# Expert mixer split by tokens: three of five token tiles go through the whole expert tables with matmuls, two tiles keep gathering their rows

## The reference

```python
def peer(h, w_q, subkeys, u_tab, v_tab):          # h: 640 tokens x 1024; u_tab, v_tab: 16384 x 1024
    q = (ht @ w_q).reshape(T, PEER_HEADS, 2, PEER_HALF)              # 8 heads x 2 x 128
    s = jnp.einsum('thpd,hpnd->thpn', q, subkeys)                    # 128 subkeys each
    s1, i1 = lax.top_k(s[:, :, 0], 16); s2, i2 = lax.top_k(s[:, :, 1], 16)
    cand = s1[..., :, None] + s2[..., None, :]; cidx = i1[..., :, None] * 128 + i2[..., None, :]
    sc, pos = lax.top_k(cand.reshape(T, 8, 256), 16)
    eidx = jnp.take_along_axis(cidx.reshape(T, 8, 256), pos, axis=-1); gate = jax.nn.softmax(sc, axis=-1)
    a = jax.nn.gelu(jnp.einsum('td,tkd->tk', xi, u_tab[ei]))         # k: 8 heads x 16 = 128 experts per token
    return jnp.einsum('tk,tkd->td', gi * a, v_tab[ei])
```

## Time and profile before

| | |
|---|---|
| median of three runs | 5233.46 us (5231.72 to 5237.55) |
| span of the profiled execution | 5232.4 us |
| granted TensorE clock, mean | 0.869 |
| bytes moved by DMA | 1482.66 MB, of them 1342.42 MB on the software queue (the gathers) |
| busy: PE, DVE, ACT, POOL | 75%, 58%, 21%, 60% |

### The profile page before, as it was taken

The page is one execution under the profiler, slowest core; times in us unless marked ns, Lnnn a source line. Parts: engine busy times, 40 slices in busy tenths (PEclk is TensorE's granted clock), DMA queues, the critical chain, the costliest instruction groups (busy, mean ns, idle before and its releaser), DMA issues. The chain is left out here.

```text
span 5232.4 us, 51066 instructions
## 1 busy us (share of the span) xinstructions
PE 3918.3 (75%) x11340; PEld 1901.7 (36%) x11340; DVE 3046.2 (58%) x6901; ACT 1093.8 (21%) x2566; POOL 3138.9 (60%) x2832
## 2 busy tenths in 40 slices
PE   8986787787787666676678898877787666766675
PEld 3544754333333222232233443533333223322232
DVE  2014744766666666666651552666666666667665
ACT  1002212212221222122211242222222221222222
POOL 0003603777777777777760331477777777777775
PEclk9998888898898888888888799888889888888888
DMA  4126017999999999999992401899999999999997
GB/s 159 58 64 175 4 36 267 387 364 361 362 362 359 354 356 358 359 357 353 356 346 77 121 1 32 315 381 365 363 363 354 359 358 364 356 353 359 357 359 302
DMA packets 525836, 1482.66 MB, mean 283 GB/s; under 512 B 52901, under 2 KB 162597, under 8 KB 525513
## 3 DMA queue, kind: packets, MB, share of 16 engines
q0 software_dynamic: 369216, 1342.42, 68.7%
q1 hardware_dynamic: 154352, 138.22, 8.2%
q10 hardware_dynamic: 2080, 0.01, 0.0%
HBM read 1476.98 MB, written 3.48 MB: 283 GB/s over the span
## 5 line engine op out<-in xcount | busy, mean ns | idle before, releaser
L1303 PE MATMUL ps<-arena,mod_scale 128*128 128x512 f32 x5120 | 2472.0, 645 | 1030.4 <-ACT mod_scale L1240 1027.8
L1303 PEld LDWEIGHTS ps<-arena,mod_scale 128*128 128x128 f32 x5120 | 1051.5, 208 | 2414.9 <-issue 2324.7
L1190 POOL DMA_INDIRECT arena<-in_peer_u,small x1280 | 1381.3, 1079 | 726.3 <-issue 377.8
L1194 POOL DMA_INDIRECT arena<-in_peer_v,small x1280 | 1503.0, 1174 | 470.1 <-issue 317.8
L1390 DVE CUSTOM_DVE_ANT_0 arena<-arena 128x1024 f32<-128x1024 f32 x1280 | 1518.2, 1223 | 412.7 <-DMA arena<-in_peer_u,small 290.7
L1240 ACT ACTIVATE mod_scale<-ident,tail 128x128 f32<-128x128 f32 x1280 | 391.4, 388 | 82.3 <-DVE tail L1400 82.3
L1400 DVE TENSOR_TENSOR tail<-tail,small 128x8 f32<-128x8 f32 x160 | 27.0, 169 | 500.6 <-ACT tail L1236 499.9
L268 POOL TENSOR_TENSOR arena<-arena 2x512 f32<-2x512 f32 x12 | 15.5, 1294 | 464.4 <-ACT arena L260 464.4
L1236 ACT ACT_TABLE_LOAD x80 | 102.6, 1283 | 864.1 <-DVE tail L1390 863.9
L1228 ACT ACTIVATE arena<-ps 128x256 f32<-128x256 f32 x80 | 30.6, 382 | 1073.7 <-PE ps L1293 1073.7
L1313 PE MATMUL ps<-hT 128*128 128x512 f32 x512 | 231.6, 606 | 11.6 <-DMA hT<-in_peer_w_q 11.6
(11 more groups left out here) (221 smaller groups left out, 3611.4 us busy)
## 6 DMA issues: line engine op xcount, KB each, us to landing
hT<-in_w_mod SPq DMA_DIRECT2D x144, 256.0 KB, 3.8
arena<-in_peer_u,small POOLq DMA_INDIRECT x1280, 6.3
arena<-in_peer_v,small POOLq DMA_INDIRECT x1280, 6.4
arena<-in_even_w_in SPq DMA_DIRECT2D x8, 2048.0 KB, 8.9
arena<-in_peer_w_q SPq DMA_DIRECT2D x8, 2048.0 KB, 11.6
hT<-in_peer_w_q SPq DMA_DIRECT2D x32, 512.0 KB, 15.0
arena<-in_w_mod SPq DMA_DIRECT2D x6, 2048.0 KB, 8.5
arena<-in_odd_w_in SPq DMA_DIRECT2D x3, 2048.0 KB, 14.1
```

Source lines behind the costliest of these rows:

```text
L1190: pool.indirect_dma_start(u_rows[:, j], None, u_table, at).then_inc(m.u_landed[j], 16)
L1194: pool.indirect_dma_start(v_rows[:, j], None, v_table, at).then_inc(m.v_landed[j], 16)
L1303: mm = pe.matmul(y_banks[b][:, c], diag[:, q, j], v_rows[:, j, c * 512:(c + 1) * 512], start=(q == 0 and j == 0), stop=(q == 1 and j == HA ...
```

## The change

Tiles 0 and 1 (256 tokens) keep the gathered way; tiles 2 to 4 (384 tokens, DENSE = 3) go through all 16384 experts. Per layer, in order:

- Queries of all five tiles are projected at the start, 16 chunks (`project`), then scored (`score`) and kept in SBUF. DVE chooses experts for tiles 0 and 1 (16 `choose`), then `decode` turns each tile's choices to indices and gates. The gathers start after decode(0).
- U pass, 128 steps in four stages of 32: SP loads expert tile i of u (128 experts, four transfers of 128 KB in pieces of 1 KB, three slots); DVE turns it with one 32x32-block transpose of 128x1024 (`turn`); PE multiplies it with hT of the 384 tokens (`dots_of`, 8 matmuls of 384 columns); ACT takes gelu and stores the 128x384 result to DRAM (`act_rows`). The model columns of u, w_q and hT are renumbered alike (`quarter`, `by_quarters`, `from_blocks`), so that the block transpose yields complete 128-row operands.
- Beside it, in stages 0 to 2 DVE chooses for tiles 2 to 4 (a head every four steps). In stages 1 to 3 the choices of a tile become a dense matrix of gates: DVE builds one-hot rows for 8 tokens (`one_hot`, two 128x1024 operations), ACT scales them (8 operations), PE multiplies them (8 matmuls of 128 columns), ACT copies the result out and stores 1 MB for each 16 tokens to DRAM (`gate_rows`); 48 such groups.
- V pass, 128 steps: SP loads v in tiles of 1 MB (two expert tiles), the stored acts (`w_in`, 768 KB for four expert tiles, pieces of 1.5 KB) and the stored gates (`g_in`, 1.5 MB for eight expert tiles, 3072 pieces of 512 B); DVE multiplies acts by gates (`weigh`, 128x384); PE accumulates 6 matmuls of 512 columns into six PSUM banks.
- The 256 picks of the gathered tiles are spread over both passes by `pace`: 1.5 per step in stage 0, 0.25 in stages 1 and 2, 1.5 in stage 3, 1.3 in the V pass; a v row follows 14 picks behind its u row. u has eight slots, v four. For tile 0 ACT scales the v row and POOL adds it; for tile 1 DVE does both in one operation (`add_row`). PE no longer takes part in them.
- The loops are written out; no register operands are left. In `modulate` of the second half the sum is written renumbered, and twice for tiles 0 and 1.

```diff
+LAG = 14
+def pace(i):
+    stage, r = divmod(i, STAGE)
+    if i < 0:
+        return 0
+    if stage == 0:
+        return max(0, 3 * (r - 1) // 2)
+    if stage in (1, 2):
+        return 45 + 8 * (stage - 1) + (r + 1) // 4
+    if stage == 3:
+        return 61 + 3 * (r + 1) // 2
+    return 109 + 13 * (i - STEPS + 1) // 10
+def picks_by(i):
+    return min(pace(i), P * GATHERED)
+def rows_by(i):
+    return max(0, min(pace(i - 1) - LAG, P * GATHERED))
...
-                        hold(pool, S.multiplied, 16 * n + 8 * q + j + 1 - SLOTS, S.pool_step)
+            pool.wait_ge(S.decoded, 1)
...
+            for k in range(PICKS + LAG):
+                if k + U_ROWS == P:
+                    pool.wait_ge(S.decoded, 2)
+                if k + U_ROWS < PICKS:
+                    pool.wait_ge(S.dotted, k + 1)
+                    u_gather(k + U_ROWS)
+                p = k - LAG
+                if p < 0:
+                    continue
...
+                elif p < P:
+                    pool.wait_ge(S.scaled, p + 1)
+                    c(pool.tensor_tensor(y_sum[:, 0], y_sum[:, 0], v_rows[:, p % V_ROWS], ALU.add))
+                else:
+                    pool.wait_ge(S.dve_added, p - P + 1)
+                if p + V_ROWS < PICKS:
+                    v_gather(p + V_ROWS)
...
+                    if g >= 2:
+                        sp.wait_ge(S.weighed, GBLOCK * (g - 1))
+                    sp.dma_start(g_in[:, g % 2].rearrange("p g i t -> p g (i t)"),
+                                 m.gate_rows[0:TG, :, g * GBLOCK:(g + 1) * GBLOCK, :].rearrange("g j i t -> j g (i t)"))\
+                        .then_inc(S.g_landed[g % 2], 16)
...
+                    if w >= 2:
+                        sp.wait_ge(S.tile_done, ABLOCK * (w - 1))
...
+                    sp.dma_start(w_in[w % 2],
+                                 m.act_rows[w * ABLOCK:(w + 1) * ABLOCK, :, 0:ND].rearrange("k j t -> j k t"))\
+                        .then_inc(S.w_in_landed[w % 2], 16)
+                if n >= 2:
+                    sp.wait_ge(S.tile_done, VBLOCK * (n - 1))
+                sp.dma_start(v_in[:, n % 2], v_dense[n]).then_inc(S.v_landed[n % 2], 16)
...
-                        mm = pe.matmul(y_banks[b][:, c], diag[:, q, j], v_rows[:, j, c * 512:(c + 1) * 512],
+                pe.wait_ge(S.u_ready, i + 1)
+                if i >= 4:
+                    pe.wait_ge(S.gelu_done, i - 3)
+                for k in range(KD):
+                    mm = pe.matmul(m.ps[:, i % 4, 0:ND], u_turned[:, i % 2, k], m.hT[:, k, N0:N], start=(k == 0),
+                                   stop=(k == KD - 1))
...
+            for k in range(TILES):
+                pe.wait_ge(S.weighed, k + 1)
+                pe.wait_ge(S.v_landed[k // VBLOCK % 2], 16 * (k // VBLOCK // 2 + 1))
+                for o in range(2 * DENSE):
+                    t, half = divmod(o, 2)
+                    mm = pe.matmul(m.ps[:, o, :], w_in[k // ABLOCK % 2][:, k % ABLOCK, t * P:(t + 1) * P],
+                                   v_in[:, k // VBLOCK % 2, k % VBLOCK, half * 512:(half + 1) * 512], start=(k == 0),
+                                   stop=(k == TILES - 1))
+                mm.then_inc(S.tile_done, 1)
...
-                    nc.scalar.activation(diag[:, q, j], m.ident[:], ACT.Copy, scale=weight[:, q, j:j + 1])\
+                nc.scalar.activation(y_sum[:, 0] if p == 0 else row, row, ACT.Copy, scale=weight[:, half % 2, j:j + 1])\
+                    .then_inc(S.scaled, 1)
...
+            def turn(i):
+                dve.wait_ge(S.u_landed[i % U_SLOTS], 64 * (i // U_SLOTS + 1))
+                if i >= 2:
+                    dve.wait_ge(S.dots_full, i - 1)
+                dve.transpose(u_turned[:, i % 2].rearrange("p c (m a) -> p m c a", m=4),
+                              u_raw[:, i % U_SLOTS].rearrange("p m (c b) -> p m c b", b=32)).then_inc(S.u_ready, 1)
...
+            def weigh(k):
+                w, g = k // ABLOCK, k // GBLOCK
+                dve.wait_ge(S.w_in_landed[w % 2], 16 * (w // 2 + 1))
+                dve.wait_ge(S.g_landed[g % 2], 16 * (g // 2 + 1))
+                to = w_in[w % 2][:, k % ABLOCK].rearrange("p (g t) -> p g t", t=STRIPE)
+                dve.tensor_tensor(to, to, g_in[:, g % 2, :, k % GBLOCK], ALU.mult).then_inc(S.weighed, 1)
...
+            for h in range(H):
+                if h == 5:
+                    turn(0)
+                    turn(1)
+                for t in range(GATHERED):
+                    choose(t, h, best[t])
+            for t in range(GATHERED):
+                decode(t, best[t])
+            for i in range(LAST):
+                if i + 2 < STEPS:
+                    turn(i + 2)
+                if i < STEPS:
+                    stage, r = divmod(i, STAGE)
+                    if stage >= 1 and r == 0:
+                        decode(GATHERED + stage - 1, best[0])
...
+                    if head_at(i) is not None:
+                        t, h = head_at(i)
+                        choose(GATHERED + t, h, best[0])
+                if STEPS - 2 <= i < 2 * STEPS - 2:
+                    weigh(i - STEPS + 2)
+                for half in halves_by(i - 2):
+                    weights(half)
+                for p in range(picks_by(i - 1), picks_by(i)):
+                    meet(p)
+                for p in range(max(P, rows_by(i - 1)), max(P, rows_by(i))):
+                    add_row(p)
```

More of the change, by code:

```diff
@@ L278, in modulate, with rows @@
     gain = m.arena[:, ARENA - D:ARENA]
+    scaled = m.arena[:, ARENA - 4 * D:ARENA - 2 * D].rearrange("p (b d) -> p b d", b=2)
+    turned = m.arena[:, ARENA - 6 * D:ARENA - 4 * D].rearrange("p (t d) -> p t d", t=GATHERED)
+    def rows(t):
+        return turned[:, t] if half == 1 and t < GATHERED else m.h[:, t]
     square = m.arena[:, ARENA - 2 * D:ARENA - D]
@@ new lines, in early, with groups_at, head_at @@
+            for q in range(4):
+                m.early.load(sp, i, slots[i][32 * q:32 * q + 32], quarter(a.peer_w_q[l], i, q))
+    return early
+STAGE = 32
+STEPS = 4 * STAGE
+def groups_at(i):
+    stage, r = divmod(i, STAGE)
+    if not 1 <= stage <= 3 or not 2 <= r < 28:
+        return range(0)
+    first = 16 * (stage - 1)
+    return range(first + 16 * (r - 2) // 26, first + 16 * (r - 1) // 26)
+def head_at(i):
+    stage, r = divmod(i, STAGE)
+    return (stage, r // 4) if stage < 3 and r % 4 == 1 else None
@@ L1196, in _ @@
-            pool.wait_ge(S.context_full, LOADS)
-            every(gathers)(pool)
-        @block.sync
-        def _(sp):
-            for n in range(2, LOADS):
-                sp.wait_ge(S.context_full, n - 1)
-                sp.dma_start(slots[n % 2], columns(a.peer_w_q[l], n)).then_inc(S.w_landed[n % 2], 16)
-            sp.wait_ge(S.context_full, LOADS)
-            sp.dma_start(w_later, w_q[:, :, 0]).then_inc(S.w_later_landed, 16)
-            with sp.Fori(1, CHUNKS) as c:
-                sp.wait_ge(S.later_full, c)
-                sp.dma_start(w_later, w_q[:, :, bass.ds(c, 1), :].rearrange("p k one n -> p k (one n)"))\
-                    .then_inc(S.w_later_landed, 16)
+            c = Chain(pool, S.chain_p)
@@ new lines, in _ @@
+            for g in range(4):
+                act.wait_ge(S.keys_full, g + 1)
+                nc.scalar.activation(keysT[:, 4 * g:4 * g + 4], m.ps[:, 4 + g, :].rearrange("p (c n) -> p c n", n=P),
+                                     ACT.Copy).then_inc(S.keys_out, 1)
+            for c in range(CHUNKS):
+                query_out(c)
+                if c >= 1:
+                    scores_out(c - 1)
+            scores_out(CHUNKS - 1)
+            softmax(0)
+            softmax(1)
+            for i in range(LAST):
+                if i < STEPS:
+                    gelu(i)
+                    if i >= 1:
+                        stage, r = divmod(i - 1, STAGE)
+                        if stage >= 1 and r == 0:
+                            choice_out(stage - 1)
+                        for n in groups_at(i - 1):
+                            gates_out(n)
+                    store_acts(i)
+                for half in halves_by(i - 1):
+                    activate(half)
+                for p in range(rows_by(i - 1), min(P, rows_by(i))):
+                    scale_row(p)
+                if i < STEPS:
+                    stage, r = divmod(i, STAGE)
+                    if stage >= 1 and r == 0:
+                        softmax(GATHERED + stage - 1)
+                    for n in groups_at(i):
+                        apply_gate(n)
```

674 lines of the change are left out of this document (382 added, 292 removed).

## The result

The changed kernel takes 5370.06 us (median of 4 runs, 5364.47 to 5375.06), the kernel before 5235.51 beside it (5231.72 to 5242.11): a ratio of 1.0259, interval 1.0244 to 1.0273. It is 2.6% slower. The forecast was 4970, and the range ended at 5260.

A forecast was written before the change was run, and what follows sets the result against it. The loops were taken as close to the DMA limit, with POOL just as near. Stretches summed to 1788 us a layer against 1924, saving 272 for two; 5232 - 272 + 6 = 4966, given as 4970, range 4760 to 5260.

The forecast's parts named there:

- Prologue, 160 us: Layer start until the steps: DVE's 16 choices set the pace after PE's first head; first gather at 143 us.
- Stages 1 and 2, 336 us: Middle of U pass: 168 us each, bound by DVE's 160 us and some imbalance; DMA engines rest.
- Stage 0, 180 us: First 32 U-pass steps: POOL, DVE and DMA near each other, DMA 170 us; taken as 180.
- Stage 3 and gap, 290 us: Last U-pass stage, 265 us with POOL's gathers and additions setting the pace, and 25 at the V pass's start.
- V pass, 810 us: 128 steps over v: DMA bytes set the pace, 49.6 us per eight expert tiles, 6.3 us a step.
- the end, 12 us: After the V pass: 12 sums of 512 and the first tiles' gates, 12 us.
- The gates: V-pass gate blocks: landing after about 33 us, DVE waiting about 10 us every eight steps, the stall just hidden.
- The bytes: Per-layer traffic: 503 MB instead of 671, 1413 us at 356 GB/s, a gain of 511 if only bytes counted.
- The turn: DVE's block transpose of each u tile in the U pass: 1.22 us taken, 2.48 the upper bound.
- rival 1: U-pass turn costs 2.48 us, strided rows being slow: +92 us a layer, 5150 us; chance 0.12.
- Rival 2: Gate blocks starve the V pass, 8.1 us a step: +230 us a layer, 5430 us; chance 0.17.
- Rivals 3 to 5: Whole kernel: DMA at 404 GB/s everywhere, 4720, chance 0.14; only bytes count, 4490, 0.04; split gains nothing, 5233, 0.04.

The follow-up runs named there:

- short queries: Changed kernel with queries of only the two gathered tiles projected, 256 of 640 columns: 5266.35 us, 1.0043 to the kernel before.
- late gates: Changed kernel with PE's and ACT's part in the gates one step later, all work kept: 5235.46 us, 0.9985 to the kernel before.
- half the dots: Changed kernel with four of the eight U-pass matmuls per expert tile left out: 5250.99 us, 1.0019 to the kernel before.
- late gates and two thirds of the picks: Changed kernel with gates' part a step later, gate loads split in four, picks one a step in stages 1 to 3: 5046.61 us, 0.9631 to the kernel before.
- gates in four parts: Changed kernel with each 1.5 MB gates load split into four of 384 KB, a cycle ahead: 5325.16 us, 1.0158 to the kernel before.

## Why the prediction was wrong

The first step that failed is a price: "PE projects a head (16 matmuls of 512 columns at 0.534 and 16 of 128 at 0.114, 10.4 us) in less than DVE's 13.2", and the same price again in "PE needs 8 matmuls of 384 columns (at 1.04 ns a column 3.2 us)" and, for the V pass, "6 x 0.534 = 3.2 us a step". The number of records was taken for the number of matmuls. Measured are 0.86 us for 512 columns and 0.645 for 384, so 5.2 us a step in either pass. At 0.6 of its price PE hid behind DVE everywhere, so no stretch was checked for what PE's order would do. That is the second step: waits between engines in order were put at nothing.

- **Prologue, 160 us: measured 213.** The first choice comes 32.6 us after the first key transpose where the forecast had 16, and then PE takes 19.5 us a head where 13.3 was taken as the pace. The short queries give back 51 of the 53 us, with the first choice at 17.0.
- **Stages 1 and 2, 336 us: measured 494.** PE is busy 206 us a stage, above the 168. With late gates and all the work there a stage takes 212 us, so 35 of the measured 247 are the order, above all PE's wait for the chain one-hot, scaling (44 us in both stages, gone with the edit). Of the 44 from 168 to 212 most is PE's work, and 15 are its waits for DVE's decode, which the edit leaves. The last section of the prediction named this as what would prove it wrong, "if DVE waits for PE's or ACT's part in the U pass, for which I allow nothing". It got no price and no chance among the rivals: PE idle 1030 us in the earlier trace rows looked like room enough.
- **Stage 0, 180 us: measured 200.** The DMA share is 0.98 at 277 GB/s, and half the dots took 14 us off. How much of the 20 is DMA and how much PE was not separated further.
- **Stage 3 and gap, 290 us: measured 272,** POOL busy 232 of them. An addition of POOL costs 2.42 us (1.9 to 3 was forecast). For a gather the forecast put the 1.06 us more of the earlier trace rows, which show it beside `meet`, on all of DVE's two-input operations; in the changed kernel a gather beside such operations took 1.27 us in the mean, and the others 0.94. POOL was not alone in setting the pace: with late gates and two thirds of the picks the stretch fell to 218.
- **V pass, 810 us: measured 780, and the end, 12 us: measured 30.** Together they are 810 where 822 was forecast. Bytes set the pass, as forecast: a cycle is 50.4 us (50 forecast). At the end PE has its last tiles still to do: DVE waits 37.8 us for them in both layers, 19 each, ahead of the sums. The forecast had no term for it.
- **The gates.** They land after a median of 21.7 us, where the forecast had 33, yet DVE stands 18.9 us for them and not about 10. The forecast took 13 ns a piece, though the 15.0 us for 1024 pieces of the earlier trace rows are 14.6, and a lead of 25 us. That a landing goes by pieces is its estimate, and no run shows it: 21.7 us are 7 ns for each of the 3072 pieces, and a load of acts that goes out between two of v landed after 11.4 us (median), 22 ns for each of its 512 pieces. The load goes out when PE has done the first four tiles of a block, and then DVE, ahead of PE, is at the block's end: the lead to DVE's need was 4.5 us in the median. The gates in four parts show what that cost, 25 us a layer.
- **The bytes.** 268 + 134 + 50 + 50 MB are 503 without the 8 MB of w_q, so the 1413 us for "503 MB with the 8 MB of w_q" are too few by 24. The sum doesn't use them.
- **The turn** costs 1.241 us; 1.22 was taken, and rival 1 (2.48 us) is out. Nor does the row behind its 2.42 ns an element (L1622) show the price of a stride: its 512 elements are written in one run, and it ran beside operations of POOL (L1588 to L1590); products of 512 elements with POOL idle (L973, L974) took 0.68 to 0.69 us. Rival 2 (gates starve the V pass) had the right sign of the result by the wrong mechanism: the V pass was faster than forecast. Rivals 3 to 5 are out as well. The chance of 0.17 for a slower kernel was nearly all rival 2's, so nothing in the forecast stood for what happened.

What the late gates leave above the forecast is 53 for the prologue and 2 x 44 for the stages, 141 us a layer: 4970 + 282 = 5252. The run measured 5235, since the other stretches happen to cancel within 10 us a layer. With PE's work as it is and the gates' part a step later, the split gains nothing; the order of the gates' part then makes the 2.6% of loss.

## What to carry to other kernels

Before a matmul is priced from a trace, count: the records of a line against the matmuls that the code issues. If there are two for one, every rate per record is half a price. Check the rate by a stretch in which a known number of matmuls runs back to back at one granted clock: here the mean of one row mixed the granted clocks 0.50 and 1.00 and gave 1.07 us where 0.86 holds at 1.00. Where a step's work goes round several engines (DVE, ACT, PE) and back, look at what stands behind the last of them in its queue: one step more of distance was worth 135 us here, as much as the whole loss. And a long wait proves no loss: of DVE's 302 us a layer at the gates an edit got back 25, because bytes filled the rest.

## What the runs showed of the hardware

- An f32 matmul is two records here (L1358: 4096 for 2048), and 512 columns took 0.86 us (1.68 ns a column) at a granted clock of 1.00, in the prologue of the changed kernel as in the earlier trace rows; 384 columns took 0.645. The forecast had 0.6 of it.
- An addition of POOL held back DVE's operations with two inputs. The one-hot operation of 128x1024 took 1.18 or 1.22 us otherwise (median); all 30 that began during such an addition ended 1.08 to 1.09 us after it and took up to 3.39 us, as if they had run only from its end. POOL's addition took 2.48 us in the mean beside such operations and 2.36 without. DVE's transposes, with one input, took 1.24 us either way. POOL's gathers in the changed kernel took 0.93 to 0.96 us where no two-input operation of DVE ran beside them (272 of them, some beside transposes), and up to 1.98 where one did.
- The 1.5 MB of gates in 3072 pieces of 512 B landed after 21.7 us (median), 7 ns a piece, with a median of 11 gathers under way for some part of that time. Mixed traffic of gathers, v, acts and gates reached 361 GB/s at a share of 0.98.
- Where PE's work in the V pass was cut to 7/12, its busy time fell by a third (679 to 446 us) and the granted clock from 0.93 to 0.78; in stage 1 with half the dots the clock fell from 0.93 to 0.81, and in the prologue with short queries from 0.94 to 0.80 (PE busy 171 to 89 us). In these three the work taken from PE did not come back in full: the mean granted clock was lower for what was left.
